# The last expert item's rows: gathered from DRAM, or placed by a product with places times gates

## What is computed

```python
def moe_ffn(h, router_w, router_b, w_gate, w_up, w_down):
    logits = (t @ router_w) + router_b
    top_vals, top_idx = lax.top_k(logits, TOP_K)          # 2 of 8 experts
    top_w = jax.nn.softmax(top_vals, axis=-1)
    gates = jnp.sum(jax.nn.one_hot(top_idx, N_EXPERTS) * top_w[..., None], axis=1)
    for e in range(N_EXPERTS):
        y = swiglu(t, w_gate[e], w_up[e], w_down[e])
        out = out + gates[:, e:e + 1] * y
...
x = rmsnorm(h + moe, final_norm_g)                          # end of the first block
...
h = rmsnorm_2(x, g_mix_norm)                                # second block
proj = jnp.einsum('bsd,de->bse', h, w_in)
sb_q, sb_k, sb_v, fx_q, fx_k, fx_v, f_logit, m_q, gate_logit = split_columns(proj, SPLITS)
```

## Time and profile before

| | us |
|---|---|
| median of 3 runs | 1998.94 |
| range of the runs | 1997.43 to 2001.46 |
| the profiled execution, its own time | 2005.06 |
| its span, first to last instruction | 2003.2 |
| PE busy | 1932.5 (96%) |
| DVE busy | 1472.3 (73%) |
| ACT busy | 1236.1 (62%) |
| mean granted clock of TensorE, share of full speed | 0.983 |

### The profile page before, as it was taken

How to read it: one execution, slowest core, us unless ns; L and a number is a source line. 1 busy time by engine, 2 the same in 40 slices (tenths; PEclk the granted TensorE clock), 3 DMA queues, 4 the chain that set the end, 5 groups by cost and what they waited for, 6 DMA issues and landing times.

```text
span 2003.2 us, 25946 instructions
## 1 busy us (share of the span) xinstructions
PE 1932.5 (96%) x9350; PEld 1605.8 (80%) x9350; DVE 1472.3 (73%) x1286; ACT 1236.1 (62%) x1085; POOL 68.4 (3%) x108
## 2 busy tenths in 40 slices
PE   7999999898999999999999999999996899999999
PEld 6888877796788888888888888888874788788887
DVE  5654656676689888988989888898885546676554
ACT  5544556322477777777777787777764457645443
POOL 0000001000100000000000000000022100000000
PEclk9999999998999999999999999999998999999999
DMA  8974533001399999999999999999984332245452
GB/s 310 365 282 147 210 144 130 1 1 74 129 415 361 383 390 361 411 364 393 363 384 392 369 402 359 391 381 371 392 314 163 142 136 87 103 147 205 176 188 83
DMA packets 76923, 521.82 MB, mean 260 GB/s; under 512 B 8240, under 2 KB 8496, under 8 KB 17584
## 3 DMA queue, kind: packets, MB, share of 16 engines
q1 hardware_dynamic: 72512, 504.02, 65.3%
q0 software_dynamic: 4192, 16.25, 2.1%
q10 hardware_dynamic: 144, 0.52, 0.1%
HBM read 501.37 MB, written 19.40 MB: 260 GB/s over the span
## 4 chain that ended last, share of the span: by engine, by line
PE 75%; DVE 5%; ACT 3%; issue 1%; POOL 1%; DMA 0%; DVEq 0%; SPq 0%; ACTq 0%; POOLq 0%
PE bank L809 15%; PE bank L810 15%; PE bank L814 15%; PE bank L506 6%; PE bank L523 6%; PE bank L507 6%; PE bank L579 4%; PE bank L831 1%; DVE w_lo L1842 1%; POOL small L1741 1%; ACT w_hi L1274 1%; DVE kT L1922 0%; PE bank L556 0%; DVE xT L1873 0%; PE bank L657 0%
## 5 line engine op out<-in xcount | busy, mean ns | idle before, releaser
L2175 DVE TENSOR_TENSOR w_lo<-raw,w_hi 128x2048 fp32r<-128x2048 f32 x336 | 762.6, 2289 | 111.3 <-ACT w_hi L1437 108.4
L1437 ACT ACTIVATE w_hi<-raw 128x2048 fp32r<-128x2048 f32 x336 | 643.4, 1919 | 143.8 <-PE bank L814 143.7
L1842 DVE TENSOR_TENSOR w_lo<-raw,w_hi 128x2048 fp32r<-128x2048 f32 (+2 forms) x136 | 298.0, 2198 | 165.9 <-ACT w_hi L1274 164.6
L1274 ACT ACTIVATE w_hi<-raw 128x2048 fp32r<-128x2048 f32 (+2 forms) x136 | 249.3, 1840 | 172.4 <-PE bank L523 159.6
L809 PE MATMUL bank<-w_hi,xT 128*128 128x512 f32 x896 | 353.8, 395 | 0.0
L810 PE MATMUL bank<-w_hi,xT 128*128 128x512 f32 x896 | 349.6, 390 | 0.0
L506 PE MATMUL bank<-w_hi,xT 128*128 128x512 f32 (+1 forms) x784 | 314.3, 402 | 20.6 <-DVE xT L1873 9.7
L507 PE MATMUL bank<-w_hi,xT 128*128 128x512 f32 (+1 forms) x784 | 308.8, 395 | 0.0
L814 PE MATMUL bank<-w_lo,xT 128*128 128x512 f32 x896 | 240.0, 390 | 0.0
L814 PEld LDWEIGHTS bank<-w_lo,xT 128*128 128x128 f32 x896 | 168.3, 188 | 35.3
L810 PEld LDWEIGHTS bank<-w_hi,xT 128*128 128x128 f32 x896 | 168.5, 188 | 33.7
(11 more groups left out here) (413 smaller groups left out, 1935.6 us busy)
## 6 DMA issues: line engine op xcount, KB each, us to landing
raw<-in_experts_dram SPq DMA_DIRECT2D x336, 1024.0 KB, 7.0
raw<-in_tiles_dram SPq DMA_DIRECT2D x125, 1024.0 KB, 4.8
rows_in<-zeros POOLq DMA_DIRECT2D x1, 6144.0 KB, 32.7
rows_out<-zeros POOLq DMA_DIRECT2D x1, 5632.0 KB, 55.3
raw<-in_tiles_dram SPq DMA_DIRECT2D x9, 512.0 KB, 3.5
item_rows<-rows_in SPq DMA_DIRECT2D x7, 512.0 KB, 7.3
rows_out<-y_s SPq DMA_DIRECT2D x7, 512.0 KB, 3.6
row<-in_rows_dram SPq DMA_DIRECT2D x1, 1040.0 KB, 14.6
```

What stands on the lines that cost most here:

```text
L1274: nc.scalar.activation(w_hi[:, i % SPL, 0:kc * w], raw[:, i % DENSE, 0:kc * w], ACT.Copy)\
L1437: nc.scalar.activation(w_hi[:, w_slot(j), :], raw[:, raw_slot(j), :], ACT.Copy).then_inc(m_hi, 1)
L1842: nc.vector.tensor_tensor(w_lo[:, i % SPL, 0:kc * w], raw[:, i % DENSE, 0:kc * w], w_hi[:, i % SPL, 0:kc * w], ALU.subtract).then_inc(spli ...
L2175: nc.vector.tensor_tensor(w_lo[:, s, :], raw[:, raw_slot(j), :], w_hi[:, s, :], ALU.subtract).then_inc(m_lo, 1)
```

## The change

Of a token's two rows, the second in item order may lie in the last item. Now no row of the last item is stored or gathered. A matrix `last_pick` (token by place in the item, holding the token's gate or zero) is made on VectorE, transposed on TensorE (`spread`), copied back (`last_spread`), and multiplied as plain fp32 with `y_s` (`last_rows`); VectorE adds the product from PSUM to `h` (`add_last`). All other rows are gathered while the last item runs, and `combine` is done inside it: six `combine` instructions of 128 x 512 at f = 5 and two in the first half of the output. A row that isn't there (its place is in the last item) is gathered from the zeroed part of `rows_out`. The head norm of mk, too, moves into the last item. In the second block the products of the right half of `h` are turned inside D1, mq's D4 is multiplied ahead of fxq's transposes, the narrow product stands after D4, and the write of the final `h` moves behind `cumf`.

```diff
@@ TensorE
+                def last_rows(c, i):
+
+                    pe.wait_ge(m_y, i * 2 + (2 + c))
+                    for tt in range(NT):
+                        b = tp_bank(("last", c, tt), "D")
+                        nc.tensor.matmul(b[:, :], last_spread[:, tt, :], y_s[:, c, :], start=True, stop=True)\
+                            .then_inc(tp_done, 1)
...
                     for j in range(5 * FB, 6 * FB):
                         f = j - 5 * FB
-                        if final and f == FB - 1:
+                        if final and f == 1:
+                            pe.wait_ge(last_placed, 1)
+                            b = tp_bank("spread", "D")
+                            for tt in range(NT):
+                                turned_pick = nc.tensor.transpose(b[:, tt * P:tt * P + P], last_pick[:, tt, :], ident)
+                            turned_pick.then_inc(tp_done, 1)
+                        if final and f == 2:
+                            result("spread")
+                            last_rows(0, i)
+                        if final and f == 4:
                             turn_norm("m2", h, (0,), (h_half, 1))
                         product(j, hidden(f), acc[3][:, :], f == 0, f == FB - 1)
...
-                tile(fxq, 0, xT1, xT2, turned="m2")
+                tile(fxq, 0, xT1, xT2, turned="m2", mid=last_half)
                 begin(fxk, "A")
-                pe.wait_ge(m_y, last_one * 2 + 3)
-                tile(fxk, 0, xT1, xT2, turned="m2")
+                between = tile_parts(fxk, 0, xT1, xT2, turned="m2")
+                next(between)
+                next(between)
+                turn_norm("m2", h, (1,), (h_half, 1, 2))
+                next(between, None)
                 turn_heads("mk")
-                turn_norm("m2", h, (1,), (h_half, 1, 2))
                 tile(fxq, 1, xT1, xT2, turned="m2")
                 tile(fxk, 1, xT1, xT2, turned="m2")
+                begin(mq, "A")
+                tile(mq, 0, xT1, xT2)
                 for c, (name, _) in enumerate(B_IN):
-                    if c > 1:
+                    if c == 2:
+                        narrow_products("forget", FORGET)
+                        tile(mq, 1, xT1, xT2)
+                        narrow_turned("forget", FORGET)
+                    elif c > 2:
                         gemm(("b_in", name), "A", xT1, xT2)
-                    if c == 2:
+                    if c == 3:
                         pe.wait_ge(fox_dve, 2)
@@ SyncE
-            ahead = 2
-            for c in range(2):
-                store_half(c)
-                for i in range(NA + (ahead if c else 0), NA + (DENSE if c else ahead)):
-                    sp.wait_ge(m_lo, last * MT + (MT - DENSE + i % DENSE + 2))
-                    load(range(i, i + 1))
+            for i in range(NA, NA + DENSE):
+                sp.wait_ge(m_lo, last * MT + (MT - DENSE + i % DENSE + 2))
+                load(range(i, i + 1))
@@ ScalarE, last item and second block
+                        if final and f == 1:
+                            head_roots("mk")
+                            act.wait_ge(y_sent, i * 16 + 16)
+                            nc.scalar.activation(small[:, 71:72], small[:, 72:73], ACT.Copy).then_inc(rows_stored, 1)
...
-                head_roots("mk")
-                split_to(NA + SPL)
                 half_squares("fin", 0, half_of(h, 0), h_sq)
                 act.wait_ge(h_gained, 1)
                 half_squares("m2", 0, gained[0], gained[0])
-                split_to(NA + SPL + 1)
+                split_to(NA + SPL)
...
-                    if c == 1:
+                    if c == 2:
                         split_to(group_of["b_in", name][1] + SPL - 1)
                         act.wait_ge(fox_dve, 1)
                         own(nc.scalar.activation(fx[:, F_E, :], fx[:, F_E, :], ACT.Exp))
@@ GpSimd
+            pool.wait_ge(rows_stored, 1)
+            collect(0, 0)
+            collect(0, 1)
+            collect(1, 0)
+            pool.wait_ge(rows_read, 1)
+            collect(1, 1)
@@ VectorE, last item and second block
+                        if final and f == 2:
+                            head_sums("mk")
+                        if final and f == 3:
+                            head_scale("mk")
+                            place_last()
+                        if final and f == 5:
+                            combine(0, 0)
+                            combine(0, 1)
+                            tell(nc.vector.memset(small[:, 70:71], 0.0), rows_read)
+                            combine(1, 0)
...
+                    if final:
+                        split_until(4 * FB + 4 + SPL)
+                        combine(1, 1)
+                        split_until(5 * FB + 1 + SPL)
+                        tell(nc.vector.tensor_copy(last_spread[:, :, :], batch("spread")[:, 0:NT * P].rearrange(
+                            "p (t r) -> p t r", t=NT)), tp_free["D"])
+                        split_until(5 * FB + 2 + SPL)
+                        add_last(0)
+                        split_until(5 * FB + 3 + SPL)
+                        gain(0)
+                        split_until(MT)
+                        norm_turn("m2", "final", halves=(0,))
...
+                add_last(1)
                 split_to(NA + 1)
-                gain(0)
+                norm_turn("m2", "final", halves=(1,))
+                gain(1)
                 split_to(NA + 3)
```

More of the change, by code:

```diff
@@ L1415, in deltanet, with head_roots @@
                 norm_turn("o", "dn_norm", 0)
+            def head_roots(name):
+                x = staged(name)
+                if name in NORMED:
+                    q = NORMED.index(name)
+                    if q:
+                        act.wait_ge(h_sq_v, q)
+                    squares_to = xn[:, :, 0:CB] if name == "mk" else head_sq
+                    for tt in range(NT):
+                        tell(nc.scalar.activation(squares_to[:, tt, :], x[:, tt * CB:tt * CB + CB], ACT.Square), h_square)
             def experts():
@@ L2164, in experts @@
                 split_to(end + 4)
+                later = rt[:, R_MAX, 4:4 + NT]
+                own(nc.vector.scalar_tensor_tensor(out=later, in0=item_f[:, 13:14].broadcast_to((P, NT)), scalar=-float(P),
+                                                   in1=to[:, :, 1], op0=ALU.mult, op1=ALU.add))
                 def start_count(signal, count):
@@ new lines, in combine @@
+            def combine(c, k):
+                for tt in range(NT):
+                    j = TOP_K * tt + k
+                    dve.wait_ge(collected[c][j], 16)
+                    hh = h[:, tt, c * CB:c * CB + CB]
+                    rows = later_rows[c][:, tt, :] if k else xn[:, tt, c * CB:c * CB + CB]
+                    own(nc.vector.scalar_tensor_tensor(out=hh, in0=rows, scalar=dest_gate[:, j:j + 1], in1=hh,
+                                                       op0=ALU.mult, op1=ALU.add))
@@ new lines, in add_last, with gain @@
+            def add_last(c):
+                for tt in range(NT):
+                    hh = h[:, tt, c * CB:c * CB + CB]
+                    tell(nc.vector.tensor_tensor(hh, batch(("last", c, tt))[:, :], hh, ALU.add), tp_free["D"])
+                tell(nc.vector.memset(small[:, 70:71], 0.0), h_half)
+            def gain(c):
+                for tt in range(NT):
+                    tell(nc.vector.tensor_tensor(gained[c][:, tt, :], h[:, tt, c * CB:c * CB + CB],
+                                                 R("final")[:, c * CB:c * CB + CB], ALU.mult), h_gained if tt else d_own)
@@ L2281, in turned @@
+                    if HEADED[name][1]:
+                        head_sums(name)
+                        head_scale(name)
                 def turned(name):
@@ L2302, in second_block @@
                     if c == 2:
-                        b = batch("cumf")
-                        tell(nc.vector.tensor_copy(fx[:, F_CUM, :], b[:, 0:16]), tp_free["D"])
-                    if c and B_IN[c - 1][0] in HEADED:
-                        turned(B_IN[c - 1][0])
-                    if c == 1:
+                        norm_used("m2")
                         wide = lambda v: fx[:, v, :].rearrange("p (t h) -> p t h", t=NT)
@@ L2319, in second_block @@
                                                             in1=fx[:, F_NLF, :], op0=ALU.mult, op1=ALU.add), fox_dve)
+                    if c == 3:
                         dve.wait_ge(fox_act, 1)
                         tell(nc.vector.tensor_tensor(fx[:, F_NLF, :], fx[:, F_M, :], fx[:, F_E, :], ALU.add), fox_dve)
+                        b = batch("cumf")
+                        tell(nc.vector.tensor_copy(fx[:, F_CUM, :], b[:, 0:16]), tp_free["D"])
+                    if c and B_IN[c - 1][0] in HEADED:
+                        turned(B_IN[c - 1][0])
                     if name in HEADED:
                         headed(name)
+                    if c == 3:
+                        for tt in range(NT):
```

(2 more changed lines are left out.)

119 lines of the change are left out of this document (45 added, 74 removed).

## The result

The changed kernel takes 2003.60 us (median of 20 runs, 2000.41 to 2007.89), the kernel before 2000.13 us (median of 20 runs, 1995.91 to 2005.76). The ratio is 1.0018 with a 95% interval of 1.0010 to 1.0025: slower by 3.6 us. Forecast was 1998.0 us, with a range up to 2003. Of the 5.6 us between forecast and result, 1.2 lie in the starting point: the forecast was made from the median of three launches, 1998.94, and twenty give 2000.13. The difference is smaller than the 4.0 us that I said could not be told; with twenty runs of each kernel it can, and its sign is not the one that I forecast.

A forecast was written before the change was run, and what follows sets the result against it. TensorE, busy 96% of the span, was taken as the bound, with gains only from its idle stretch at 1500 us on. +4.2 - 5.6 - 0.9 + 1.2 + 0.2 = -0.9 us off 1998.94 gave 1998.0 us, range 1992 to 2003.

The forecast's parts named there:

- the low clock: TensorE at 1.2 GHz behind long waits: 1.7 to 3.1 us at D1, up to 1.5 between D2 and D8.
- The item: Last expert item: VectorE's delay 2.2, spread 0.2 and 2.0, fp32 products 1.8, less 1.9 saved: +4.2 us.
- The smaller additions: Last item, f = 1 to 3: 1.3 us on ScalarE, 1.4 and 1.8 us on VectorE, said to cost nothing.
- From the item's end to D2: Item's end to D2's end: 36.0 us before, 28.0 at full clock, 30.4 with low clock, a gain of 5.6 us.
- From D2 to D8: D2's end to D8's start: 47.2 us before, 46.3 us after with VectorE setting the pace, a gain of 0.9 us.
- the chain of fxq: From D2's end through fxq's and fxk's norms and splits to the narrow product's copy: 25.7 us; TensorE stalls 5.9 us.
- The second leg: From the forget transposes through mq's norm to D8's and D9's splits: 18.3 us against TensorE's 12.1, a 6.2 us wait.
- The price weighed against a rule: ScalarE's table load for the forget gates: 1.28 us by the trace row, 2.66 us by the skill page; row taken.
- D8: Tile D8 may run at the low clock behind the 6.2 us wait: 0 to 2 us, taken as 1.2.
- the one through the clock: Three six-microsecond waits each followed by 3.1 us of low clock, 4.9 us over the sum, 2003; chance 0.10.
- The rival through the gathers: Gathers in the last item delay weight tiles or stall VectorE: +4 us over the sum, 2002 to 2003; chance 0.07.
- the rival of the vanished idle time: Idle time of 1500 to 1560 us goes without a successor: about -20 us, 1979; chance 0.04.

The follow-up runs named there:

- D1's split: Changed kernel with VectorE splitting D1 and D2 directly behind D0's split, ahead of the right half's turn and gain: 1.0002 of the kernel before.
- the gain early: Changed kernel with the right half's gain on VectorE and squares on ScalarE ahead of that half's turn: 1.0003 of the kernel before.
- the kernel with all edits: Changed kernel with item work moved to VectorE's idle places, D1's and D2's splits, gain and forget instructions early: 1975.39 us, 0.9877 of the kernel before.
- the forget edit: Changed kernel with the narrow product's copy and the forget instructions placed ahead of splits in VectorE's list: 0.9960 of the kernel before.

## Why the prediction was wrong

The mechanism was right for each wait of TensorE that I named; the sum came out at -0.9 us and is +3.43. The waits that I forecast in TensorE's list, and what was there: 1.5 us at tile 24 and 2.23; 0.7 us at f = 6 and none (0.53 and 0.50 in two executions with D1's split and with the gain early); 2.0 us ahead of the fp32 products and 1.88; D0 1.5 and 1.45; D1 6.6 and 6.53; ahead of the forget transposes 5.9 and 6.38; ahead of `cumf` 6.2 and 3.81. The steps that failed are the size of two terms, VectorE's delay in the item and the low clock, and one path: the chain through GpSimd's root, which the sum left out.

**The item: +4.2 forecast (its terms add up to 4.3), +6.57 measured.** "The smaller additions ... cost nothing": they cost 0.72 us at f = 3 (from one set of transposes to the next 12.09 us instead of 11.37; scaling and places take VectorE 2.1 us), 0.39 of it as a wait. They also used up VectorE's lead. I had the two splits at f = 5 come 3.9 us later than before; they came 5.3 us later (1451.41 - 567.85 = 883.56 us behind the mark, before 1450.30 - 572.06 = 878.24), while TensorE was 0.9 us later itself, so the wait is 2.23 instead of 1.5 us. Behind it the clock was low, which I had charged only to waits of 6 us: 4.46 us from low part to low part instead of 2.72, 1.74 us. Only half of that is lost, though. In the two executions in which the clock stayed high there (D1's split and gain early) TensorE waited 0.53 and 0.50 us at f = 6, about the 0.7 us that I had forecast, and D0 came 939.93 and 939.94 us behind the mark instead of 940.79. So the low clock hid the wait at f = 6 and costs 0.86 us net, and 1.5 of the 2.4 us by which this term was short are VectorE's. The rest was right: 4.13 us for the spread and the products (4.0), and 2.4 us saved by the wait for `h` that went (1.9).

**From the item's end to D2: -5.6 forecast, -5.57 measured.** The two waits are as forecast, and so is the low clock behind D1's: its low part takes 3.78 us against 1.98. For the low clock I had added 2.4 us; from D1's low part to D2's it is 8.41 us here and 6.82 in the kernel with D1's split early, which has no such wait, so it is 1.6. Other terms were 0.8 us short, and the exact sum is luck to that extent.

**From D2 to D8: -0.9 forecast, +0.50 measured.** I let the chain of fxq begin at D2's end (the end of the record of its low part, 1537.22 + 1.98). It began 0.9 us later, since ScalarE's copy waits for the root of `m2`, and I had not worked out when this root ends. My own row of before showed the wait, 3.89 us for L1815 at 1543.94. The rows of ScalarE and GpSimd:

```profile
1540.10 1.41 ACT L1572 ACTIVATE xn<-bank,small 128x512 f32<-128x512 f32 x2 [5.50 <-POOL small L1838]
```

```profile
1528.08 0.72 POOL L1774 TENSOR_TENSOR small<-small 128x2 f32<-128x2 f32 x1 [73.56 <-ACT gained L1322]
1528.90 2.11 POOL L1775 TENSOR_SCALAR small<-small 128x2 f32<-128x2 f32 x1
1531.09 0.72 POOL L1763 TENSOR_TENSOR small<-small 128x2 f32<-128x2 f32 x1
1531.89 0.19 POOL L1764 TENSOR_TENSOR small<-small 128x2 f32<-128x2 f32 x1
...
1535.14 2.12 POOL L1765 TENSOR_TENSOR small<-small 128x2 f32<-128x2 f32 x1
1537.35 2.11 POOL L1766 TENSOR_SCALAR small<-small 128x2 f32<-128x2 f32 x1
1539.54 0.19 POOL L1767 TENSOR_TENSOR small<-small 128x2 f32<-128x2 f32 x1
1539.81 0.20 POOL L1838 TENSOR_TENSOR small<-small 128x2 f32<-128x2 f32 x1
```

The right half's gain stands on VectorE behind the turn, its squares on ScalarE behind that, and the root begins only at 1528.08 and takes until 1540.01, 11.9 us. In the kernel before it took 5.6:

```profile
1538.24 0.20 POOL L1752 TENSOR_TENSOR small<-small 128x2 f32<-128x2 f32 x1 [15.75 <-ACT gained L1304]
...
1543.65 0.19 POOL L1815 TENSOR_TENSOR small<-small 128x2 f32<-128x2 f32 x1
```

The experiments with the gain and with D1's split show that this chain is a bound of its own: each edit alone gave some 4 us and both gave 9.6. The second leg was 18.2 us long (1565.94 to 1584.12) where I had 18.3, but TensorE's own part of it ran at the low clock, so its wait is smaller (3.81 us) and the sum the same. The low clock went on behind it: `cumf` and mq's heads took 2.8 us where I had 1.3, and I had taken 1.0 us of low clock for the whole chain, at most 1.5.

The price weighed against a rule came out by the row. The exp and ln of the forget gates:

```profile
1567.53 1.28 ACT L1587 ACT_TABLE_LOAD   x1 [15.45 <-DVE small L2376]
1568.83 0.22 ACT L1587 ACTIVATE small<-small 128x16 f32<-128x16 f32 x1
1569.06 1.28 ACT L1588 ACT_TABLE_LOAD   x1
1570.36 0.21 ACT L1588 ACTIVATE small<-small 128x16 f32<-128x16 f32 x1
```

Each activation follows its load of 1.28 us after 0.02 us. The Trainium skill's figure for the drain ("ScalarE: Activation LUTs", "What ACT_TABLE_LOAD costs") doesn't appear here either; had it been right, the second leg would have been 2.8 us longer than measured.

**D8: +1.2 forecast, +1.93 measured**, within the 0 to 2 that I gave. Its ten first matmuls are spaced by 0.43 us instead of 0.23.

The rival that comes nearest is the one through the clock, at 0.10. Its condition, that D8 runs low behind the third wait, came about; but of the 4.3 us between -0.9 and +3.43 only 0.9 (item, net) and 1.2 (heads and D8 beyond what my sum had) are the clock's, and the rest are mainly VectorE's lead (1.5) and the root (0.9). The rival through the gathers is out: no wait of TensorE or ScalarE between f = 3 and D8 ends with a landing, although the first gathers were issued at 1419.5 us beside the weight stream. And the rival of the vanished idle time, which I gave 0.04, failed for the reason named, the order of the lists: in the kernel with all edits that order is mended, the waits are gone without successors, and it is 24 us faster than the kernel before by the trace. What the kernel before would gain from an order of its own was not tried.

## What to carry to other kernels

When a change takes a long wait out of an in-order engine, write down for each helper's list what now stands ahead of the next small instruction that the main engine needs: here splits of 2.2 us stood ahead of copies of 0.2 to 0.4 us, and cost 13 us. Follow every chain that starts at the moved point, not only the one of the last releaser: an edit on one of two nearly equal chains shows only the difference to the other (4 us each, 9.6 together). And charge the low clock to waits of 2 us too, as a chance; what it costs in the end is less than it takes (1.7 us taken, 0.9 lost here) where another wait stands behind it.

## What the runs showed of the hardware

Waits of TensorE of 2.23 to 2.27 us were followed by the granted clock of 1.2 GHz in four of six executions. Of eleven waits of 1.87 to 1.95 us (eight ahead of the fp32 products, one in the kernel before, one each in the kernels with the forget edit and with all edits) two were, nine were not. Behind the waits of 5.9 us and more it was low each time: D1's low part took 3.67 to 3.78 us instead of 1.98 behind waits of 6.53 and 6.54 us. What decides at 2 us is open.

GpSimd's instructions on 128 x 2 elements take 0.19 us, but 2.11, 2.12 and 2.11 us at 1528.90, 1535.14 and 1537.35 in the rows above. VectorE at these times:

```profile
1526.46 4.50 DVE L1865 TENSOR_TENSOR w_lo<-raw,w_hi 128x2048 fp32r<-128x2048 f32 x2
...
1534.91 4.49 DVE L1865 TENSOR_TENSOR w_lo<-raw,w_hi 128x2048 fp32r<-128x2048 f32 x2
```

Two splits each, 1526.46 to 1530.96 and 1534.91 to 1539.40: the long instructions end within 0.1 us of the end of a split, and the instructions of 0.19 us lie where VectorE makes no split. In the kernel before VectorE made no split beside this root, and it took 5.6 us; here it takes 11.9. My sum took the lengths of the head roots from rows of before and would have been no better for this one. This is how the Trainium skill describes it ("SBUF — State Buffer", section "🔬 SBUF: two separate sides"): the port pair that VectorE and GpSimd share is locked for a whole instruction, and against a GpSimd operation that reads SBUF VectorE takes it also for operations with two inputs in SBUF, as a split is. The trace agrees: GpSimd's instruction is held until the split is over (2.11 us instead of 0.19), not slowed in proportion. No run here takes the splits away from beside this root and changes nothing else, so the port as the cause is read from these times and from the page.
